# The experts' biases as three exact 16-bit parts, added by 16-bit products with a one-hot pick

## The reference

```
gu = lax.ragged_dot(xs, w_gate_up, group_sizes) + b_gate_up[e_sorted]
gate, lin = jnp.split(gu, 2, axis=-1)
gate = jnp.minimum(gate, SWIGLU_LIMIT)
lin = jnp.clip(lin, -SWIGLU_LIMIT, SWIGLU_LIMIT)
act = (lin + 1.0) * (gate * jax.nn.sigmoid(SWIGLU_ALPHA * gate))
out = lax.ragged_dot(act, w_down, group_sizes) + b_down[e_sorted]
```

## Time and profile before

| | us |
|---|---|
| median of three runs (2565.17 to 2568.31) | 2567.62 |
| span of the profiled execution | 2566.9 |
| TensorE busy | 2471.5 (96%) |
| VectorE busy | 1506.3 (59%) |
| ScalarE busy | 1226.7 (48%) |
| GpSimd busy | 329.9 (13%) |
| DMA, mean over the span | 209 GB/s |

### The profile page before, as it was taken

One profiled execution on the slowest core, in us unless ns is written; L12 is line 12 of the kernel. 1 busy time (PEld: TensorE's weight loads), 2 busy tenths in 40 slices (PEclk: granted clock), 3 DMA queues, 4 the chain that ended last, 5 costly groups with the idle time before them and its releaser, 6 DMA issues.

```text
span 2566.9 us, 41888 instructions
## 1 busy us (share of the span) xinstructions
PE 2471.5 (96%) x14427; PEld 1980.3 (77%) x14428; DVE 1506.3 (59%) x1486; ACT 1226.7 (48%) x1246; POOL 329.9 (13%) x379
## 2 busy tenths in 40 slices
PE   8999999999999989976999999999999999999996
PEld 7987777998888878974788777777777886778775
DVE  4312333332333235355789876888876997688877
ACT  6413444220112021064577665666655775667665
POOL 0000000000000000042121212121121221212110
PEclk9999999999999999997999999999999999999998
DMA  4133243224332212447789987898977997899988
GB/s 129 34 50 54 66 73 80 49 50 49 50 50 81 99 66 91 146 167 263 257 317 384 371 296 257 319 381 287 369 252 258 376 381 271 306 335 331 387 278 304
DMA packets 262285, 536.68 MB, mean 209 GB/s; under 512 B 28952, under 2 KB 79896, under 8 KB 261120
## 3 DMA queue, kind: packets, MB, share of 16 engines
q1 hardware_dynamic: 241184, 488.96, 57.3%
q0 software_dynamic: 21024, 46.65, 6.7%
HBM read 492.92 MB, written 42.63 MB: 209 GB/s over the span
## 4 chain that ended last, share of the span: by engine, by line
PE 51%; DMA 1%; DVE 1%; issue 0%; ACT 0%; POOL 0%; ACTq 0%; POOLq 0%; DVEq 0%
PE m_y L2158 5%; PE m_gate L2158 5%; PE m_gate L2162 4%; PE m_lin L2158 4%; PE m_gate L2160 4%; PE m_lin L2162 4%; PE m_lin L2160 4%; PE m_y L2160 4%; PE m_y L2162 4%; PE m_spill L2200 4%; PE m_turn L2212 2%; PE m_turn L2150 1%; PE m_gate L2168 1%; PE m_y L2168 1%; PE m_spill L2196 1%; PE m_lin L2168 1%
## 5 line engine op out<-in xcount | busy, mean ns | idle before, releaser
L1973 DVE TENSOR_TENSOR m_w_lo<-raw,m_w_hi 128x2048 fp32r<-128x2048 f32 x384 | 874.6, 2288 | 253.7 <-ACT m_w_hi L1847 234.8
L1847 ACT CAST m_w_hi<-raw 128x2048 fp32r<-128x2048 f32 x384 | 733.3, 1911 | 446.2 <-PE m_lin L2162 230.1
L106 PE MATMUL c_bank<-h_hi_r,ring_hi 128*128 128x512 f32 x640 | 251.7, 393 | 0.9 <-PEq L396 0.9
L108 PE MATMUL c_bank<-h_lo_r,ring_hi 128*128 128x512 f32 x640 | 249.5, 390 | 0.0
L109 PE MATMUL c_bank<-h_hi_r,ring_raw_r 128*128 128x512 f32 x640 | 249.2, 389 | 0.0
L147 ACT CAST ring_hi<-ring_raw 128x2048 fp32r<-128x2048 f32 x43 | 82.1, 1908 | 280.4 <-DMA ring_raw<-in_w_in 128.3
L2158 PE MATMUL m_gate<-m_w_hi,m_x_hi 128*128 128x512 f32 x512 | 209.6, 409 | 0.0
L2158 PE MATMUL m_y<-m_w_hi,m_a_hi 128*128 128x512 f32 x512 | 206.1, 403 | 1.5 <-DVE m_a_lo L2025 1.5
L2162 PE MATMUL m_gate<-m_w_hi,m_x_lo 128*128 128x512 f32 x512 | 201.1, 393 | 0.0
L2160 PE MATMUL m_y<-m_w_lo,m_a_hi 128*128 128x512 f32 x512 | 201.0, 393 | 0.0
L2158 PE MATMUL m_lin<-m_w_hi,m_x_hi 128*128 128x512 f32 x512 | 200.7, 392 | 0.0
(11 more groups left out here) (336 smaller groups left out, 4539.9 us busy)
## 6 DMA issues: line engine op xcount, KB each, us to landing
raw<-in_w_gate_up SPq DMA_DIRECT2D x512, 512.0 KB
raw<-in_w_down SPq DMA_DIRECT2D x256, 512.0 KB, 12.3
ring_raw<-in_w_in SPq DMA_DIRECT2D x31, 1024.0 KB, 9.4
gates<-work POOLq DMA_DIRECT2D x32, 256.0 KB, 2.6
work<-gates SPq DMA_DIRECT2D x8, 1024.0 KB, 7.2
v<-in_x SPq DMA_DIRECT2D x8, 512.0 KB, 12.5
ring_raw<-in_w_branch_b SPq DMA_DIRECT2D x4, 1024.0 KB, 5.3
ring_raw<-in_w_branch_a SPq DMA_DIRECT2D x4, 1024.0 KB, 5.2
```

The costliest lines, as they stand in the source:

```text
L106: pe.matmul(out, left_hi(k), right_hi(k), start=first and k == kts[0], stop=False, skip_group_check=True)
L108: pe.matmul(out, left_hi(k), right_lo(k), start=False, stop=False, skip_group_check=True)
L1847: act.copy(w_hi[:, p % WS].rearrange("p k b n -> p (k b n)"), raw[:, raw_slot(m)].rearrange("p k b n -> p (k b n)")).then_inc(signals.whi, 1)
L1973: dve.tensor_tensor(w_lo[:, p % WS].rearrange("p k b n -> p (k b n)"), raw[:, raw_slot(m)].rearrange("p k b n -> p (k b n)"), f32(w_hi[:, ...
```

## The change

`b_split` becomes a 16-bit (bf16) tile of 128 x 3072, with gate-up in columns 0 to 2047 and down in 2048 to 3071, and `pick` becomes bf16. The biases are loaded, in full width, into partitions 0 to 31, 64 to 95 and 96 to 127; partitions 32 to 63 are cleared, and `base` gives them no expert. Each of the three copies becomes one part of the bias: the first rounding, the rounding of what is left, and the rounding of what is left then. This needs two more casts on ACT and, on DVE, subtractions that write back into `b_raw`. One pick now serves both kinds of bias and `base` has one column. The products of L2168, L2196 and L2207 are as many and as large as before, and their operands have 16 bits.

```
-            for quarter in range(NG):
+            for quarter in PARTS:
                 held_by = slice(E * quarter, E * (quarter + 1))
-                if quarter < 2:
-                    sp.dma_start(b_raw[held_by, :], b_gate_up).then_inc(b_loaded, 16)
-                else:
-                    sp.dma_start(b_raw[held_by, 0:F], b_down).then_inc(b_loaded, 16)
+                sp.dma_start(b_raw[held_by, 0:2 * F], b_gate_up).then_inc(b_loaded, 16)
+                sp.dma_start(b_raw[held_by, 2 * F:3 * F], b_down).then_inc(b_loaded, 16)
...
-            pool.memset(b_raw[2 * E:P, F:2 * F], 0.0).then_inc(b_cleared, 1)
+            pool.memset(b_raw[E:2 * E, :], 0.0).then_inc(b_cleared, 1)
...
             act.wait_ge(b_raised, 1)
             act.copy(b_split[:, :], b_raw[:, :]).then_inc(b_rounded, 1)
             for n in range(O + 2, END):
                 ring.split_hi(act, n)
+                act.wait_ge(b_left, n - O - 1)
+                under = slice((n - O) * E, P)
+                act.copy(b_split[under, :], b_raw[under, :]).then_inc(b_rounded, 1)
             for i in range(TT):
                 square(i)
...
-                    dve.tensor_scalar(b_raw[0:2 * E, F:2 * F], b_raw[0:2 * E, F:2 * F], 1.0, None, ALU.add) \
+                    dve.tensor_scalar(b_raw[:, F:2 * F], b_raw[:, F:2 * F], 1.0, None, ALU.add) \
...
-                if n == O + 1:
-                    dve.wait_ge(b_rounded, 1)
-                    for low_part in (slice(E, 2 * E), slice(3 * E, 4 * E)):
-                        dve.tensor_tensor(b_split[low_part, :], b_raw[low_part, :], f32(b_split[low_part, :]),
-                                          ALU.subtract)
+                if n > O:
+                    dve.wait_ge(b_rounded, n - O)
+                    under = slice((n - O + 1) * E, P)
+                    dve.tensor_tensor(b_raw[under, :], b_raw[under, :], b_split[under, :], ALU.subtract) \
+                        .then_inc(b_left, 1)
...
-        pick = sb("pick", [P, 2, P], F32R)
+        pick = sb("pick", [P, 2, P], BF16)
...
-                dve.tensor_scalar(pick[:, a, :], cst["base"][:, a:a + 1].to_broadcast([P, P]),
+                dve.tensor_scalar(pick[:, a, :], cst["base"][:, :].to_broadcast([P, P]),
...
-                    bias(p_y[0][:, :], 1, 0)
-                    bias(p_y[1][:, :], 1, NW)
+                    bias(p_y[0][:, :], 1, 2 * F)
+                    bias(p_y[1][:, :], 1, 2 * F + NW)
...
-                        right = f32(b_split[:, :]).rearrange("p (b j n) -> p b j n", b=2, j=2)
-                        pe.matmul(into(g), f32(pick[:, 0, 0:SPILL]), right[:, :, j, P * g:P * g + P], start=True,
+                        right = b_split[:, 0:2 * F].rearrange("p (b j n) -> p b j n", b=2, j=2)
+                        pe.matmul(into(g), pick[:, 0, 0:SPILL], right[:, :, j, P * g:P * g + P], start=True,
...
-                        pe.matmul(p_turn[SPILL * g:SPILL * (g + 1), 0:256], f32(pick[:, 1, 0:SPILL]),
-                                  f32(b_split[:, 256 * g:256 * g + 256]), start=True, stop=False,
+                        pe.matmul(p_turn[SPILL * g:SPILL * (g + 1), 0:256], pick[:, 1, 0:SPILL],
+                                  b_split[:, 2 * F + 256 * g:2 * F + 256 * g + 256], start=True, stop=False,
...
-            expert_f, b_split = late("expert_f", [P, W]), late("b_split", [P, 2 * F], F32R)
+            expert_f, b_split = late("expert_f", [P, W]), late("b_split", [P, 3 * F], BF16)
```

More of the change, by code:

```diff
@@ L88 @@
 SLOT = 2 + 2 * NG
+PARTS = (0, 2, 3)
 GATE_MAX = LIMIT / (1.0 + math.exp(-ALPHA * LIMIT))
@@ L265, in _ @@
             step(pool.memset(cst["base"][:, :], -1.0))
-            for quarter in range(NG):
+            for quarter in PARTS:
                 held_by = slice(E * quarter, E * (quarter + 1))
-                step(pool.tensor_scalar(cst["base"][held_by, quarter // 2:quarter // 2 + 1], cst["part"][held_by, :],
+                step(pool.tensor_scalar(cst["base"][held_by, :], cst["part"][held_by, :],
                                         float(-E * quarter), None, ALU.add))
@@ L1111, in output_and_route @@
         terms, ones = sb("terms", [EX, 4 * W + 1]), sb("ones", [EX, P])
-        b_raw = sb("b_raw", [P, 2 * F])
+        b_raw = sb("b_raw", [P, 3 * F])
         turned = [psum(f"turned{s}", [P, D]) for s in range(2)]
@@ L1119, in output_and_route @@
         m_hi_done, m_lo_done, ready, taken = sem("m_hi_done"), sem("m_lo_done"), sem("ready"), sem("taken")
-        b_cleared, b_loaded, b_raised, b_rounded = sem("b_cleared"), sem("b_loaded"), sem("b_raised"), sem("b_rounded")
+        b_cleared, b_loaded, b_raised = sem("b_cleared"), sem("b_loaded"), sem("b_raised")
+        b_rounded, b_left = sem("b_rounded"), sem("b_left")
         listed, blanked, cleared, scaled = sem("listed"), sem("blanked"), sem("cleared"), sem("scaled")
@@ L1273, in _ @@
             ring.split_hi(act, O + 1)
-            act.wait_ge(b_loaded, 16 * NG)
+            act.wait_ge(b_loaded, 32 * len(PARTS))
             act.wait_ge(b_raised, 1)
@@ L1363, in _ @@
                 if n == O:
-                    dve.wait_ge(b_loaded, 16 * NG)
-                    dve.tensor_scalar(b_raw[0:2 * E, F:2 * F], b_raw[0:2 * E, F:2 * F], 1.0, None, ALU.add) \
+                    dve.wait_ge(b_loaded, 32 * len(PARTS))
+                    dve.tensor_scalar(b_raw[:, F:2 * F], b_raw[:, F:2 * F], 1.0, None, ALU.add) \
                         .then_inc(b_raised, 1)
@@ L2352, in decoder_block @@
         cst = {"ident": sb(whole, "ident", [P, P]), "iota": sb(whole, "iota", [P, P]),
-               "base": sb(whole, "base", [P, 2]),
+               "base": sb(whole, "base", [P, 1]),
                "eps": sb(whole, "eps", [P, 1]), "part": sb(whole, "part", [P, 1])}
```

## The result

The kernel with the change takes 2553.21 us (median of 4 runs, 2551.45 to 2554.68), the one before 2566.84 us in the same session (4 runs, 2565.17 to 2568.31): a ratio of 0.995 [0.9938, 0.9962], 13.6 us or 0.5% faster. The forecast was 2552.9 us.

What follows compares the result with a forecast made beforehand. PE's stream was taken to bound the expert stage, unless DMAs are late. The terms -12.5 - 1.7 - 3.3 + 2.8 = -14.7 us took the 2566.9 us span to 2552.2, median 2552.9 us; 8-in-10 range 2548 to 2561.

Steps and rivals of the forecast that it cites:

- Step 1: Overflow biases in the expert stage: 39 groups fall from 0.45 to 0.13 us each, gaining 12.5 us (9.0 to 13.3).
- The rival that gave 9.0: Overflow biases: bf16 strips run no faster than a 32-bit round, gain 9.0 us, kernel at 2559.7 us; chance 20%.
- Step 2: Main bias products of 512 columns themselves: 0.012 us saved on each of 145, 1.7 us (0 to 3).
- the rival built on it: Main picks much faster, at about 131 ns spacing: 19 us less, kernel at 2535 us; chance 2%.
- Step 3: Main biases behind overflow products, 47 places: faster bf16 weight loads save 0.07 us each, 3.3 us (0 to 4.5).
- The stop belongs to the width and not to the type: On PE, changing the tile's width stops the array, changing operand type does not; the change keeps all tiles.
- The slower rival: Type changes around picks stop PE after all, losing 31.4 us, kernel at 2589 us; chance 8%.
- My sign for it: On PE: an fp32r product beginning more than 0.25 us behind a pick would show the prediction wrong.
- Step 4: Preparing the bias parts up to output panel O+2: wider cast and subtraction are hidden, no cost.
- Step 5: Preparing the parts between output panels O+2 and O+3: router's first logits come later, cost 2.8 us (0.7 to 5).
- Step 6: Making the picks on DVE: as many, of the same 128 x 128, so no change.
- Loads: Rival in the expert stage: DMA loads take the gain back, 2559 to 2562 us if half were lost; chance 5%.

Runs made afterwards that it cites:

- c_over32: c_after with only the overflow biases added by plain 32-bit products again (their values wrong), main biases still 16-bit: 2565.37 us, ratio 1.0002 to the kernel before.
- c_before_pair: The kernel before, 32-bit biases kept, with the overflow's gate-up panels taken two at a time: 2548.64 us, ratio 0.9923 to the kernel before.
- c_early: c_after with DVE's bias subtractions moved from behind a panel's last tile to behind its second, the last cast following early: 2556.1 us, ratio 0.9945.
- c_castlate: c_after with only ACT's last bias cast moved behind the router's eight tiles, DVE's subtraction left in place: 2556.83 us, ratio 0.9947 to the kernel before.
- c_after: The changed kernel with one more register operation on each value read from the plan of supers: 2557.36 us, ratio 0.9954 to the kernel before.
- c_quadback: c_early with overflow gate-up panels four at a time and DVE's next-super pick behind the second x_lo, ahead of the activation: 2527.24 us, ratio 0.9835.
- c_quadmid: c_early with overflow gate-up panels four at a time and DVE's next-super pick behind x_lo and activation, ahead of w_lo: 2548.66 us, ratio 0.9934.
- c_before: The kernel before with one more register operation on each value read from the plan of supers: 2570.15 us, ratio 1.0.
- c_quadlate: c_quadmid with DVE's next-super gate-up pick one w_lo later, behind that w_lo: 2619.61 us, ratio 1.0203 to the kernel before.

## Why the prediction was right, step by step

- *Step 1, overflow biases.* Forecast 12.5 (9.0 to 13.3), measured 13.0, and shown by taking this part back (c_over32). Four bf16 strips do run side by side at one pass, 0.119 us a group against an estimate of 0.13. The rival that gave 9.0 is refuted. The Trainium skill, "TensorEngine Tiling (Array Packing)", section Restrictions, would have held the loads up; if it does so for 32-wide tiles, it costs nothing visible here, since the whole group of four fits in 0.12 us (a load's record is 0.093 us long for these 32 columns, and 0.096 for the 128 of the main picks).
- *Step 2, main picks.* Mis-sized: 1.7 forecast, 0.7 measured for the 49 picks behind main panels. The 16-bit picks of 512 columns are 0.230 us apart (1320.32 to 1320.55), as the fp32r ones were. The Trainium skill, "TensorE: Matmul & The Clock Gate", section Back-to-back issue gap, gives 131 ns for this spacing; the trace does not agree, and the rival built on it is refuted.
- *Step 3, main picks behind overflow.* Mis-sized the other way: 3.3 forecast with 4.5 as the bound, 5.5 measured. I had put the saving at 0.07 us; it is 0.12: the record falls from 0.50 to 0.39 us, the usual length, and with it more than the 0.10 us beyond the usual step that I took for the uncovered load. The load's own record fell from 0.187 to 0.096 us. Steps 2 and 3 together: 5.0 forecast, 6.2 by the records and 5.2 by the stage length in c_over32.
- *The stop belongs to the width and not to the type.* Right. No type change at 128 x 128 costs anything (two steps of 0.44 us behind the picks), plain 32-bit turns between fp32r products cost nothing either, and c_before_pair gives the width's price without any 16-bit pick. The slower rival, 2589 us, is refuted. My sign for it, a product that begins more than 0.25 us behind a pick, could not have decided, since that stamp comes at 0.03 us; two steps taken together do.
- *Step 4, hidden preparation.* From the first product of this stage to the last addition of O+2 it is 69.4 us before (1019.36 to 1088.77) and after (1024.11 to 1093.52). The wider cast and subtraction of 2.75 and 3.36 us delay nothing there.
- *Step 5, preparation at the turn.* Forecast 2.8, measured 2.8, and split by c_early and c_castlate in 0.9 and 1.9. The clock did fall in the profile after (0.73, logits 3.60 us), so there the step cost 4.5 us, near its upper bound of 5; in c_after, with the same instructions on PE, the logits took 1.93 us, so it is not in every execution.
- *Step 6, picks.* Right: 64 before and after, of 0.28 us each. One pick would serve both kinds of bias now, but the kernel still makes two in a super.
- *Loads.* No part of the gain was given back there. ACT's waits for the gate-up loads in the profile after, against the earlier trace rows:

```profile
ACT m_w_hi L1850 <- DMA raw<-in_w_gate_up: 7.7, 7, 1.6
```

The sum forecast -14.7; its parts measured in the traces give -18.2 + 2.8 = -15.4, and the medians -13.6. The stages that the forecast left out moved by more (+4.8 before the output stage, some -5 for the router's stall) than its error, so the mechanism is borne out by the stage lengths and the experiments, and the closeness of 2552.9 to 2553.21 is in part luck. In the chances is a slip: the parts given for faster add up to 0.87 and those for the same to 0.05, not 0.85 and 0.07.

## What to carry to other kernels

Where small biases start sums in column strips, a 16-bit product in exact parts costs a quarter of the 32-bit one (0.119 and 0.453 us for a group of four). But the larger price is the change of the tile's width: 0.3 us for each block, in and out, where fp32r products follow it, and some 0.2 where a 16-bit one does. Count the blocks and gather them. Before a block is moved, list what each operand's next writer has queued behind it, in the iterations without the block as well.

## What the runs showed of the hardware that was not expected

- Behind a bf16 product of 512 columns the record of the next fp32r product starts 0.03 us after it and is 0.58 us long. Behind the plain 32-bit turns of the kernel before it is the same (0.03 and 0.31 us, 71 places). Single distances between starts mislead there; sums over two steps don't.
- The way out of the strips costs less before a bf16 product: gate pick record 0.39 us and follower at 0.23 us, where a following fp32r product has 0.50 and 0.33.
- In some kernels the router has a stall: DVE begins an addition 3.0 us after PE has ended the last product of its bank (1116.63 in c_quadback). ACT and PE follow DVE by 0.46 and 0.48 us, as they do without the stall, so only DVE is late. Here is c_quadback's; in c_quadmid DVE goes on from the same place in 0.6 us:

```profile
1116.71 0.25 ACT L1265 COPY g_low<-g_p_low 32x128 f32<-32x128 f32 x1 [0.79 <-remote]
...
1119.63 0.42 DVE L1306 TENSOR_TENSOR h_hi<-g_bank,h_hi 128x256 f32<-128x256 f32 x1 [3.51 <-remote]
...
1120.11 1.97 PE L1444 MATMUL g_turned<-ident,h_hi 128*128 128x128 f32 x8 [2.85 <-issue]
```

  It is in the profiles of before, c_before, c_after, c_early, c_castlate and c_quadback, not in those of the other seven, and in five of the six it is followed by products at half speed (the 8 turns take 1.94 to 1.97 us instead of 1.09), in c_castlate not. Its cause is open: no run was made for it. Less the 0.9 or 2.8 us of the turn, these six take 84.5 to 87.3 us from the last addition of O+2 to the first turn of the experts' tokens. Five of the other seven take 80.3 to 80.6 (the kernel after less its slow logits too), two 82.3 and 82.5. Against the five the stall with the slow products is worth 4 to 7 us, more than step 5.
- Each of the 18 stalls of PE in c_quadlate (4.06 us from start to start, 3.67 of them idle) was followed by products 0.38 to 0.43 us apart instead of 0.23, for 2 to 3 us in most places and for some 5 in four: a wait on PE costs more than its length once the clock falls. The stalls of 1.86 us in c_quadmid (1.47 idle) were not followed by such products.
